# Attention stage of a hybrid encoder kernel: conv diagonals on GpSimd, first taps and scaled maxima on ScalarE

## The reference

```python
proj = jnp.einsum('bsd,de->bse', hn, w_in)         # q (8 heads x 64), k, v (2 x 64), u (2 x 512)
q = apply_rope(rms_norm(q, q_g), cos, sin)
k = apply_rope(rms_norm(k, k_g), cos, sin)
a_out = block_attention(q, k, v)                   # softmax(q k / 8) v, 4 query heads per k/v head
u = u[..., :CONV_CH] * jax.nn.sigmoid(u[..., CONV_CH:])
u = depthwise_conv(u, conv_w) + conv_b             # 512 channels, width 31, centred
c_out = jax.nn.silu(layer_norm(u, cln_g, cln_b))
mix = jnp.concatenate([a_out, c_out], axis=-1)
return jnp.einsum('bse,ed->bsd', mix, w_out)
```

## Time and profile before

| | |
|---|---|
| median of 3 runs | 1361.47 us (1361.33 to 1363.37) |
| the profiled execution | 1361.89 us, its span 1360.1 us |
| PE busy | 1335.8 us (98%) |
| VectorE busy | 1156.1 us (85%) |
| ScalarE busy | 1008.5 us (74%) |
| GpSimd busy | 46.9 us (3%) |

### The profile page before, as it was taken

One profiled execution on the slowest core, in us unless ns is written; L12 is line 12 of the kernel. 1 busy time (PEld: TensorE's weight loads), 2 busy tenths in 40 slices (PEclk: granted clock), 3 DMA queues, 4 the chain that ended last, 5 costly groups with the idle time before them and its releaser, 6 DMA issues.

```text
span 1360.1 us, 19059 instructions
## 1 busy us (share of the span) xinstructions
PE 1335.8 (98%) x6747; PEld 1126.5 (83%) x6747; DVE 1156.1 (85%) x1241; ACT 1008.5 (74%) x1188; POOL 46.9 (3%) x55
## 2 busy tenths in 40 slices
PE   7999999999999999999999999999999999999998
PEld 6868999988778888888888888888888888888886
DVE  6986555557799999999999999999999999999995
ACT  6866444446788887888888788888878888888874
POOL 1000000000050000000000000000000000000000
PEclk9999999999999999999999999999999999999999
DMA  9407853376799899999999999999999999999930
GB/s 350 163 1 272 301 186 124 125 250 235 110 379 397 309 394 395 374 360 396 394 339 394 395 374 359 396 395 339 394 395 374 359 396 394 394 393 398 400 122 33
DMA packets 178484, 427.03 MB, mean 314 GB/s; under 512 B 4096, under 2 KB 13568, under 8 KB 178432
## 3 DMA queue, kind: packets, MB, share of 16 engines
q1 hardware_dynamic: 173248, 412.10, 80.9%
q0 software_dynamic: 3168, 11.54, 3.3%
q10 hardware_dynamic: 2016, 2.72, 0.6%
HBM read 419.53 MB, written 6.82 MB: 313 GB/s over the span
## 4 chain that ended last, share of the span: by engine, by line
PE 91%; DVE 5%; ACT 2%; issue 1%; DMA 0%; SPq 0%; ACTq 0%; DVEq 0%
PE G L1366 18%; PE G L1368 18%; PE G L1367 18%; PE Y L1366 11%; PE Y L1368 11%; PE Y L1367 11%; PE G L1712 2%; DVE lo_ring L803 2%; DVE ring L863 1%; DMA ring<-in_w_in 0%; ACT xT_hi L504 0%; ACT tok L561 0%; DVE xT_lo L833 0%; ACT hi_ring L468 0%; DVE s_small L934 0%
## 5 line engine op out<-in xcount | busy, mean ns | idle before, releaser
L803 DVE TENSOR_TENSOR lo_ring<-ring,hi_ring 128x1024 fp32r<-128x1024 f32 x692 | 838.3, 1224 | 141.6 <-ACT hi_ring L468 100.1
L468 ACT ACTIVATE hi_ring<-ring 128x1024 fp32r<-128x1024 f32 x692 | 732.8, 1062 | 250.5 <-PE G L1368 149.0
L1366 PE MATMUL G<-hi_ring,xT_hi 128*128 128x512 f32 x896 | 353.9, 395 | 1.4 <-DVE lo_ring L803 0.8
L1368 PE MATMUL G<-lo_ring,xT_hi 128*128 128x512 f32 x896 | 349.5, 390 | 0.0
L1367 PE MATMUL G<-hi_ring,xT_lo 128*128 128x512 f32 x896 | 348.8, 389 | 0.0
L1366 PE MATMUL Y<-hi_ring,mT_hi 128*128 128x512 f32 x568 | 223.9, 394 | 0.0
L1368 PE MATMUL Y<-lo_ring,mT_hi 128*128 128x512 f32 x568 | 221.3, 390 | 0.0
L1367 PE MATMUL Y<-hi_ring,mT_lo 128*128 128x512 f32 x568 | 221.2, 389 | 0.0
L1366 PEld LDWEIGHTS G<-hi_ring,xT_hi 128*128 128x128 f32 x896 | 168.2, 188 | 36.0 <-DVE lo_ring L803 2.0
L1368 PEld LDWEIGHTS G<-lo_ring,xT_hi 128*128 128x128 f32 x896 | 168.3, 188 | 35.8
L1367 PEld LDWEIGHTS G<-hi_ring,xT_lo 128*128 128x128 f32 x896 | 168.4, 188 | 33.5
(11 more groups left out here) (251 smaller groups left out, 939.6 us busy)
## 6 DMA issues: line engine op xcount, KB each, us to landing
ring<-in_moe_wg SPq DMA_DIRECT2D x56, 2048.0 KB, 11.8
ring<-in_moe_wu SPq DMA_DIRECT2D x56, 2048.0 KB, 13.3
ring<-in_moe_wd SPq DMA_DIRECT2D x56, 2048.0 KB, 13.2
ring<-in_ffn_wg SPq DMA_DIRECT2D x5, 2048.0 KB, 11.5
ring<-in_ffn_wu SPq DMA_DIRECT2D x5, 2048.0 KB, 10.1
ring<-in_ffn_wd SPq DMA_DIRECT2D x5, 2048.0 KB, 7.9
ring<-in_ple_gate_w SPq DMA_DIRECT2D x4, 2048.0 KB, 7.8
ring<-in_w_out SPq DMA_DIRECT2D x2, 2048.0 KB, 13.4
```

What stands on the lines that cost most here:

```text
L468: act.activation(hi_ring[:, n % AHEAD, :], where, ACT.Copy).then_inc(hi_done, 1)
L803: dve.tensor_tensor(lo_ring[:, n % AHEAD, :], where, hi_ring[:, n % AHEAD, :].bitcast(F32), ALU.subtract).then_inc(lo_done, 1)
L1366: pe.matmul(dst, s_hi, m_hi, start=start, stop=False, skip_group_check=True)
L1368: return pe.matmul(dst, s_hi, m_lo, start=False, stop=stop, skip_group_check=True)
```

## The change

1. GpSimd makes all 36 diagonals, by `tensor_scalar` on the identity, behind the rotary tables: nine as soon as the constants are there, the other 27 behind `qk_rot`. ScalarE's calls of `diagonals` go, among them its wait for `qk_rot`.
2. ScalarE makes tap 0 of tiles 0, 1 and 2 with one activation each (`first_tap`). Those of tiles 0 and 1 come behind the gate product `glu_done` 1, in the input projection; that of tile 2 comes in step 0 of the loop, behind the two exponentials of head 0.
3. VectorE no longer makes any tap 0. `EARLY_ROWS` goes from 16 to 17, so the early list holds taps 1 to 16 of tiles 0 and 1 (32 taps, as before), and the late list 53 taps in place of 56.
4. VectorE ends a head's maximum with the reduction, which now signals `max_done`; there is no wait behind it. ScalarE makes the two scaled negative maxima of the head (128x1 each) ahead of the exponentials, and waits for its own results.

```diff
-EARLY_ROWS = 16
+EARLY_ROWS = 17
-EARLY_TAPS = tuple((c, k) for k in range(EARLY_ROWS) for c in range(2))
+EARLY_TAPS = tuple((c, k) for k in range(1, EARLY_ROWS) for c in range(2))
-                   + [((k + 0.4) / SHARED, (2, k)) for k in range(SHARED)])
+                   + [((k + 0.4) / SHARED, (2, k)) for k in range(1, SHARED)])
...
     @block.scalar
-        def diagonals(last):
-            while made[0] < min(last, len(PE_TAPS)):
-                c, k = PE_TAPS[made[0]]
-                act.activation(diag_of(made[0]), ident, ACT.Copy, scale=conv_w[:, c, k:k + 1]).then_inc(diag_a, 1)
-                made[0] += 1
+        def first_tap(c):
+            act.activation(conv[:, c, :], upad[:, c, 0:SEQ], ACT.Identity, bias=conv_b[:, c:c + 1],
+                           scale=conv_w[:, c, 0:1]).then_inc(conv_v[c], 1)
...
-        for n in range(3, 7):
-            hi_upto(n + AHEAD)
-            diagonals(3 * (n - 3))
+        hi_upto(3 + AHEAD)
+        act.wait_ge(glu_done, 1)
+        first_tap(0)
+        first_tap(1)
+        hi_upto(6 + AHEAD)
...
-        act.wait_ge(qk_rot, 1)
-        diagonals(EARLY_DIAGS + 6)
...
         for i in range(HEADS + 2):
             if i < HEADS:
-                act.wait_ge(neg_done, i + 1)
+                act.wait_ge(max_done, i + 1)
                 for t in range(T):
+                    act.activation(s_small[:, 44 + 2 * (i % 2) + t:45 + 2 * (i % 2) + t],
+                                   s_small[:, 40 + 2 * (i % 2) + t:41 + 2 * (i % 2) + t], ACT.Copy,
+                                   scale=qk_scale[:, 20 + t * 10 + i:21 + t * 10 + i]).then_inc(neg_done, 1)
+                for t in range(T):
+                    act.wait_ge(neg_done, T * i + t + 1)
                     act.activation(prob[:, i % 2, t, :], ..., ACT.Exp, ...).then_inc(exp_done, 1)
-            diagonals(EARLY_DIAGS + 6 + 4 * (i + 1))
+            if i == 0:
+                act.wait_ge(glu_done, 2)
+                first_tap(2)
...
     @block.vector
         def tap(c, k):
-            if k == 0:
-                dve.tensor_scalar(conv[:, c, :], upad[:, c, 0:SEQ], ...).then_inc(conv_v[c], 1)
-            else:
-                dve.wait_ge(conv_v[c], k)
-                ...
+            dve.wait_ge(conv_v[c], k)
+            ...
...
-                link(dve.tensor_reduce(s_small[:, 40 + 2 * b:42 + 2 * b], ..., ALU.max))
-                dve.tensor_tensor(s_small[:, 44 + 2 * b:46 + 2 * b], s_small[:, 40 + 2 * b:42 + 2 * b], nqk[:, i, :],
-                                  ALU.mult).then_inc(neg_done, 1)
+                dve.tensor_reduce(s_small[:, 40 + 2 * b:42 + 2 * b], ..., ALU.max).then_inc(max_done, 1)
...
     @block.gpsimd
+        pool.wait_ge(vec_in, 16)
+        for n, (c, k) in enumerate(PE_TAPS):
+            if n == EARLY_DIAGS:
+                pool.wait_ge(qk_rot, 1)
+            pool.tensor_scalar(diag_of(n), ident, conv_w[:, c, k:k + 1], None, ALU.mult).then_inc(diag_a, 1)
```

More of the change, by code:

```diff
@@ L314, in kernel_program @@
     table_set, q_sq, k_sq, k_zero = sem("table_set"), sem("q_sq"), sem("k_sq"), sem("k_zero")
-    sc_done, neg_done, exp_done, nrm_done = sem("sc_done"), sem("neg_done"), sem("exp_done"), sem("nrm_done")
+    sc_done, max_done, neg_done, exp_done, nrm_done = sem("sc_done"), sem("max_done"), sem("neg_done"), sem("exp_done"), sem("nrm_done")
     sum_inv = sem("sum_inv")
@@ L512, in _ @@
         act.dma_start(qk_gain, a["qk_gain"].broadcast_to([P, 2 * HEAD_DIM])).then_inc(qk_gain_in, 16)
-        made = [0]
-        def diagonals(last):
-            while made[0] < min(last, len(PE_TAPS)):
-                c, k = PE_TAPS[made[0]]
-                act.activation(diag_of(made[0]), ident, ACT.Copy, scale=conv_w[:, c, k:k + 1]).then_inc(diag_a, 1)
-                made[0] += 1
+        def first_tap(c):
+            act.activation(conv[:, c, :], upad[:, c, 0:SEQ], ACT.Identity, bias=conv_b[:, c:c + 1],
+                           scale=conv_w[:, c, 0:1]).then_inc(conv_v[c], 1)
         hi_upto(2 + AHEAD)
@@ L857, in tap @@
         def tap(c, k):
-            if k == 0:
-                dve.tensor_scalar(conv[:, c, :], upad[:, c, 0:SEQ], conv_w[:, c, 0:1], conv_b[:, c:c + 1],
-                                  ALU.mult, ALU.add).then_inc(conv_v[c], 1)
-            else:
-                dve.wait_ge(conv_v[c], k)
-                dve.scalar_tensor_tensor(out=conv[:, c, :], in0=upad[:, c, k:k + SEQ], scalar=conv_w[:, c, k:k + 1],
-                                         in1=conv[:, c, :], op0=ALU.mult, op1=ALU.add).then_inc(conv_v[c], 1)
+            dve.wait_ge(conv_v[c], k)
+            dve.scalar_tensor_tensor(out=conv[:, c, :], in0=upad[:, c, k:k + SEQ], scalar=conv_w[:, c, k:k + 1],
+                                     in1=conv[:, c, :], op0=ALU.mult, op1=ALU.add).then_inc(conv_v[c], 1)
         early, late = list(EARLY_TAPS), list(LATE_TAPS)
@@ L927, in o_low @@
             dve.tensor_tensor(mT_lo[:, c, :], G[:, c % 2, 0:SEQ], mT_hi[:, c, :].bitcast(F32), ALU.subtract).then_inc(o_lo, 1)
-        nqk = qk_scale[:, 20:40].rearrange("p (t n) -> p n t", t=T)
         for i in range(HEADS + 2):
@@ L933, in _ @@
                 dve.wait_ge(sc_done, i + 1)
-                link(dve.tensor_reduce(s_small[:, 40 + 2 * b:42 + 2 * b], Y[:, b, :].rearrange("p (t n) -> p t n", t=T), AX.X, ALU.max))
-                dve.tensor_tensor(s_small[:, 44 + 2 * b:46 + 2 * b], s_small[:, 40 + 2 * b:42 + 2 * b], nqk[:, i, :],
-                                  ALU.mult).then_inc(neg_done, 1)
+                dve.tensor_reduce(s_small[:, 40 + 2 * b:42 + 2 * b], Y[:, b, :].rearrange("p (t n) -> p t n", t=T), AX.X,
+                                  ALU.max).then_inc(max_done, 1)
             if i >= 2 and i % 2 == 0:
```

## The result

The changed kernel's median is 1366.27 us (1364.21 to 1366.68, six runs), against 1361.42 us (1361.10 to 1363.37) for the kernel before on the same chip; the ratio on record is 1.0027, its 95% interval 1.0017 to 1.0038 (the two medians by themselves are 1.0036 apart; the ratios below too are those on record and not the quotients of medians). The profiled execution took 1365.48 us with a span of 1363.5 us. As the experiments show, about half of this difference is chance in the first 18 us of the executions; on equal terms the change costs 2.3 us, 1364.05 us against 1361.72 us.

The account below looks back on a forecast made before the run. PE carries 91% of the chain, but in attention PE, VectorE and ScalarE lie close, so waits decide. +0.94 to head 7's reciprocal, -0.15 at the end, +0.2 contention: +1.0 us, put at 1362.5 us, range 1361.0 to 1365.8.

Parts of the forecast that it names:

- step 0, wait and scaled maxima, to the reciprocal of head 0: First loop step: tap (2,1) waits for ScalarE's first tap of tile 2, so head 0's reciprocal comes 1.15 us later.
- odd steps: Loop steps 1, 3, 5, 7: the exponentials end last, scaled maxima lengthen each by 0.09 us, +0.36 us for four.
- even steps: Loop steps 2, 4, 6: VectorE ends last, so the product's 0.19 us is won in each, -0.57 us for three.
- taps beside GpSimd in steps 0 and 1: First two loop steps: no loss forecast; the 27 late diagonals needed 10 us from about 47.0.
- GpSimd beside the 18 taps: Taps from 48.15 us: each loses 0.09 us to GpSimd's diagonals; less 1.4 us of slack, +0.2 us.
- end: VectorE's chain to PE's: Attention's end: three taps fewer give only 0.15 us, then ScalarE's copy, waiting for PE, ends last; -0.15 us.
- The idle time I had asked the profile to show: Sign near 59.5 us: VectorE idle 0.4 to 0.8 us ahead of tap (2,1), released by ScalarE.
- The 0.8 for four that stood in brackets: Loop steps 1, 3, 5, 7: +0.8 us in all if a head's two scaled maxima run one behind the other.
- rival (1): Taps from 48.15 us: GpSimd's reads cost 0.22 us a tap, 4.0 us less 1.4 slack; 1364.9 us, chance 0.27.
- Rivals (2): VectorE is the bound throughout, so its 2.7 us come off: 1358.8 us, chance 0.07.
- (3): GpSimd is starved beside VectorE's two-input instructions; about 11 diagonals left for the end, +4 us: 1366 us, chance 0.04.

Follow-up runs that it names:

- on equal terms: Changed kernel and kernel before, each with four extra PE matmuls ahead of the first transposes: 1364.05 us against 1361.72 us.
- ScalarE's diagonals: Changed kernel with ScalarE making the diagonals again, in the places it had before: stage 58.24 us, median 1365.22 us, ratio to before 1.0010.
- the writes-only run: Changed kernel with GpSimd writing zeros by memset in place of the 36 diagonals, matmul taps left out: stage 58.17 us, median 1363.39 us, ratio 1.0010.
- the four matmuls: Kernel before with four unused 128x128 by 256-column PE matmuls ahead of the first transposes: median 1361.72 us, ratio 0.9993, times in one group.

## Why the prediction was right where it was, and wrong in a size

The median of six, 1366.27 us, lies 0.5 us above the stated range of 1361.0 to 1365.8; 1361.4 times the ratio 1.0027 is 1365.1 and lies in it, and so does the time on equal terms, 1364.05 us, 2.3 us above before where +1.0 was forecast. That is under the 0.2% named for a change that can be told; it could be told only once the two groups were one. The direction was right and so was the mechanism, at these sizes:

| step | forecast | measured |
|---|---|---|
| step 0, wait and scaled maxima, to the reciprocal of head 0 | +1.15 | +1.45, of it 0.19 contention |
| odd steps | 4 x +0.09 | 4 x +0.17 |
| even steps | 3 x -0.19 | 3 x -0.20 |
| taps beside GpSimd in steps 0 and 1 | none | +0.48 and +0.29 |
| GpSimd beside the 18 taps | +0.2 | 0, hidden |
| end: VectorE's chain to PE's | -0.15 | -0.10 |
| sum | +1.0 | +2.2 |

- **Step 0.** Right in place and releaser. 24.09 - 22.64 = 1.45 us on the reciprocal, counted from 38.25 and 36.70. ScalarE's diagonals leave 1.26 (62.49 - 38.59 against 22.64), so the steps priced at 1.15 measure 1.26: the first tap takes 0.59 us and not 0.50, the scaled maxima 0.37 and not 0.33. The idle time I had asked the profile to show, 0.4 to 0.8 us, was a slip: it is 2.23, for it takes in the old wait.
- **Odd steps.** The exponentials do end last, and the step grows. Mis-sized: the two scaled maxima of a head take 0.46 to 0.48 us together and the first exponential starts behind both, 0.39 us after the first of them began. The 0.8 for four that stood in brackets was the better price.
- **Even steps and the end.** As forecast, both. The spared taps became 0.99 us of idle time ahead of L925, which is the 1.2 us less the 0.15 and a little. VectorE's lower busy time (1155.9 us against 1156.1) was no measure of anything.
- **GpSimd.** This is the step that failed. I took a diagonal at 0.37 us from rows of 16 and 64 elements, at 1.3 ns an element; it takes 0.58 us from start to start by itself and 0.70 on average. With 27 of them until 67.6 us, the contention fell where VectorE has no slack, in steps 0 and 1, and the stretch for which I had priced it, with 1.4 us of slack, lost 0.3 us and hid it (ScalarE starts head 0 21.42 us behind the rotation's start in both kernels). The 0.9 to 1.0 us that ScalarE's diagonals give back are most of the gap between +1.0 and +2.2; the scaled maxima's 4 x 0.08 are the next part.
- **The rule on the port.** The Trainium skill (page "SBUF — State Buffer", section "Who interferes with whom") has a VectorE instruction with two SBUF inputs contend with a GpSimd one that reads SBUF and not with one that only writes; the writes-only run agrees for the seven taps that had memsets beside them. The same page of the Trainium skill, section "Summary: rules for kernel authors", has the second of the two to issue blocked until the first finishes. That does not hold here: beside diagonals of 0.58 us a tap loses 0.02 to 0.19 us. So rival (1) was right in kind and, in the loop, near in price (0.16 to 0.19 us a tap against its 0.22); it was wrong in its place, for beside the 18 taps, where it put the whole, a tap loses 0.02 us.
- **Rivals (2) and (3)** fell: VectorE's spared 2.7 us did not come off, and no wait of PE ended with GpSimd.

## What to carry to other kernels

Work taken off the busiest engine is worth what the chain at that place says, head by head: here one product was worth 0.20 us in the steps where VectorE ended last and cost 0.17 us in those where ScalarE did, and three spared taps at the end were worth 0.1 us since PE's chain lay 0.15 us behind. When an operation moves to another engine, look up what stands in front of its first consumer in that engine's queue; a sorted list puts it elsewhere than one thinks, and a small shift moves the wait rather than removing it. GpSimd beside VectorE taps is not free if it reads SBUF: price how long it goes on, and see whether that end still lies under slack.

## What the runs showed of the hardware

- PE's first matmuls on weights, at 13 us, had a pitch (start to start) of 0.213 us for 3.5 to 5.0 us in five profiles and of 0.12 in the others, with a granted clock of 1.00 in the rows of both; 256 columns in 0.213 us are 1.2 GHz, the lower of the clock's two levels. In all the profiles without the four matmuls PE had idled until 7.8 to 8.3 us and made 16 transposes from then to 12.5 at the latest; what selects the pitch there isn't shown. With four matmuls from 5.4 us on, 32 of 33 times of three kernels lay in the earlier group (the other, 1362.70 us, may). This is worth 1.5 us of the median here, and it puts the rotation of one profile up to 2.35 us later than that of another (38.89 against 36.54).
- A GpSimd `tensor_scalar` of 128x128 f32 with a scalar from SBUF takes 0.58 us from start to start with VectorE idle or in step with it, 0.83 beside back-to-back taps, and 1.3 to 1.8 beside a low-half subtraction; a memset of that size 0.15. The first one showed no extra time (1.57 us, the second 1.64, both beside subtractions), though the first `tensor_scalar` of the kernel before took 5.50 us.
- Taps and GpSimd's reads fall into one of two rhythms: one read for two taps, at which a tap loses 0.02 us, or one for one, at which it loses 0.16 to 0.19. What selects the rhythm stays open: the changed kernel had the second from 62 us on, the kernel with GpSimd's diagonals alone had the first beside its 18 taps and something between in the loop (0.04 to 0.05 us a tap).
